# Latent projection stage with its weights loaded a stage early and eight output buffers; unused matmuls at stage borders

## The chip, the core and the metric

The kernel runs on one core of a Trainium2 chip. That core has five engines with instruction streams of their own (TensorE, called PE in the profile; VectorE, DVE; ScalarE, ACT; GpSimd, POOL; SyncE, SP, which only issues transfers), an on-chip memory of 128 partitions (SBUF), a small memory that matmuls write into (PSUM), and DMA engines between SBUF and DRAM. Engines wait for each other through semaphores. The metric is the device time of one execution in microseconds (us).

## The reference

Two transformer stacks of two layers run one after the other on one sequence of 1024 tokens, width 1024. The first has a differential attention layer, a recurrent (gated linear) layer and a squared-ReLU MLP after each. The second has two "mixed" layers, each a sum of three mixers behind one projection `h @ w_in`: retention, latent attention (MLA) and gated linear attention (GLA). What the change touches is the latent attention:

```python
q = (rms_norm(q_lat, q_norm_w) @ w_uq).reshape(b, s, MLA_HEADS, MLA_NOPE + MLA_ROPE)   # 8 heads, 64 + 32
q_nope, q_pe = q[..., :64], rope_2(q[..., 64:], pos)
kv = (rms_norm(kv_lat, kv_norm_w) @ w_ukv).reshape(b, s, MLA_HEADS, MLA_NOPE + MLA_V)
k_nope, v = kv[..., :64], kv[..., 64:]
k_pe = rope_2(k_rope[:, :, None, :], pos)[:, :, 0, :]
sc = (q_nope @ k_nope + q_pe @ k_pe) * 96 ** -0.5
mask = key_chunk[None, :] <= q_chunk[:, None]            # chunks of 64 tokens
p = softmax(where(mask, sc, -inf)); out = p @ v
```

## The kernel before

Activations lie transposed: `xT` is eight tiles of 128 channels x 1024 tokens, in SBUF all the time. The program is a row of stages: `attention_layer` (tag `da`), `trunk` (`tk`: the rest of the first stack), then for each of the two mixed layers `mixed_front` (`pj`), `mla_project` (`mp`) and `mixed_back` (`ma`), and at the end `final_norm` (`n`). Each stage allocates its buffers and semaphores with `stage(...)` and ends with a barrier over all engines (L78), so nothing of a stage starts before the last engine of the one before it, SP with its awaited stores among them, is done. Inside a stage each engine's order is written out by hand.

**`mla_project`, the stage changed most.** SP first issues the loads of `wq` (768 KB), `wk` and `wv` (256 KB each), then the rope tables and the rows of `k_rope`. PE waits for all three weights (`pe.wait_ge(sems["w"], 48)`), and then makes ten outputs of 128 x 1024 in the order `[4, 5, 0, 1, 2, 3, 6, 7, 8, 9]` into the two halves of one PSUM tile: 4 and 5 are q's rope parts, 0 to 3 q's other parts (each two plain float32 matmul steps by two halves of 512 tokens, twenty-four matmuls in all), 6 to 9 k's (one step by two halves, eight matmuls). After these come eight matmuls for v. Each float32 matmul shows as two records in the trace. ACT copies every output out of PSUM: the first two into `ab`, the next eight into `o`, and v's into `v`. `o` has two buffers, so before output number `at` >= 4 ACT waits until the stores of `at - 2` have landed (`st0`, `st1`). SP stores each output as two transfers of 64 partitions (256 KB each). After the sixth output (`at == 5`) SP waits for DVE's rotation of q's and k's rope parts and issues four more stores (two of 512 KB, two of 64 KB) before it goes on with `at` 6 to 9. At the end SP waits for all stores. `mixed_back` reads them back from DRAM.

**`mixed_back`, its first microseconds.** SP loads q (96 rows), k (64 rows) and the shared `mkpe` (32 rows) of the first pair of heads, and so on. Rows 96 to 103 of each tile hold the mask: POOL clears them for q, then for k (two memsets of 8 x 4096); DVE then writes -1e30 into q's and 1 into k's by a product with eight columns of the identity (8 instructions of 8 x 512 in all). PE's first score matmul waits for all eight (`mask` >= 8) and for the loads (`landed0`).

**`mixed_front`.** DVE scales the identity by 1/rms of each token (L386), PE multiplies that with ones to spread it over all partitions (`prep.tensor`, L355: two float32 matmuls of 512 columns), DVE then makes the normalised tiles (L403, L415) and ACT their rounded part (L337). The weights arrive in 22 panels of 512 KB through `pn.raw`, two buffers, loaded by SP (L145) and split by POOL in two parts (L160, L162, later L1183, L1185). In the second mixed layer eight column sums with one column each precede (L344), and ACT's stream begins with eight stores of `xT` and two loads. In the first the sums come from the trunk's end (L811): 16 such column sums, after DVE's last addition, before ACT and DVE make `norms` from them.

**`trunk`.** Its first panel product waits for the low parts of `oT` (L979), tile by tile.

Of the kernel before, what the change touches and what calls it, by code (L numbers as in the profile page):

```python
# [13 lines left out]
ACT = mybir.ActivationFunctionType  # L14
# [258 lines left out]
class Prep:  # L273
# [6 lines left out]
    def __init__(self, model, sems, sb, ps, chunks, size=1, eps=None, whole=False, mul=1.0, shift=None, scale=None,  # L280
                 mode="split", gates=None, sums=None, room=None, t=None, psum=None, given=None, also=None):
        self.m, self.sems, self.chunks, self.size, self.eps = model, sems, chunks, size, eps
        self.given, self.also = given, also
# [56 lines left out]
    def tensor(self, pe):  # L340
        m, sems = self.m, self.sems
        if self.whole and self.given is None:
            for b in range(SB):
                last = pe.matmul(self.stat[:, b:b + 1], m.acc[:, b * P:(b + 1) * P], m.ones[:, 0:1], start=True,  # L344
                                 stop=True)
            last.then_inc(sems["h_sums"], 1)
        for s, c in enumerate(self.normed[:1] if self.whole else self.normed):
# [9 lines left out]
            last.then_inc(sems["h_spread"], 1)  # L357

# [107 lines left out]
class Model:  # L466
# [30 lines left out]

    @contextmanager
# [42 lines left out]
    def final_norm(self, tag, name, mode):  # L541
        nc = self.nc
        with stage(nc, tag, PREP_SEMS + ["sq", "acc"]) as (sems, sb, ps):
            prep = self.norm_prep(name, 0, mode=mode)(sems, sb, ps)
# [78 lines left out]
    def trunk(self, oT, held):  # L623
# [13 lines left out]
        with stage(nc, "tk", names) as (sems, sb, ps):  # L637
# [27 lines left out]
            with nc.Block() as block:  # L665
# [62 lines left out]
                def _(pe):  # L728
# [60 lines left out]
                    pn.credit(pe)  # L789
                    linear(W_O, lambda k: pe.wait_ge(sems["o_lo"], k + 1))  # L790
# [15 lines left out]
                    mlp(1, MLP[1], 2)  # L806
                    pe.wait_ge(sems["acc"], 36)
# [5 lines left out]
                    last.then_inc(sems["n_sums"], 1)  # L813

# [287 lines left out]
    def mixed_front(self, tag, w, layer, v, o_ret, o_gla, al, make):  # L1102
# [13 lines left out]
            "l_cs", "l_kt", "l_kn", "l_s", "l_at", "l_state", "l_sm", "l_u", "l_o", "l_oc", "l_qb", "l_root", "l_rn"]  # L1116
# [4 lines left out]
        with stage(nc, tag, PANEL_SEMS + names) as (sems, sb, ps):  # L1121
# [3 lines left out]
            aux = ps("aux", [P, 2, S])  # L1125
            given = dict(given=self.norms[:, 1, :], also=self.col("fin_g", 0, DK)) if layer == 0 else {}
            prep = make(sems, sb, ps, room=ab[:, 1, 0:1, :], t=ab[:, 0, :, :], psum=aux, **given)
            pn = Panels(nc, sems, sb, ps, w, N_PROJ, DK, prep, n_v, v_parts, acc)
            decay = sb("decay", [P, 4, P])
# [32 lines left out]
            with nc.Block() as block:  # L1162
                @block.sync
                def _(sync):
# [5 lines left out]
                    pn.load(sync)  # L1170

# [39 lines left out]
                def _(pe):  # L1211
# [11 lines left out]
                    pn.credit(pe)  # L1223
                    prep.tensor(pe)
# [289 lines left out]
                def _(dve):  # L1514
# [170 lines left out]
    def mla_project(self, tag, layer, v):  # L1685
        nc = self.nc
        names = ["w", "link", "acc", "out", "st0", "st1", "tab", "kpe", "rot", "rot_st"]
        with stage(nc, tag, names) as (sems, sb, ps):
# [4 lines left out]
            wq = sb("wq", [P, 6, 2, P])  # L1693
            wk = sb("wk", [P, 4, P])
            wv = sb("wv", [P, 512])
            o = sb("o", [P, 2, S])
            acc = ps("acc", [P, 2, S])
            order = [4, 5, 0, 1, 2, 3, 6, 7, 8, 9]
            with nc.Block() as block:
                @block.sync  # L1700
                def _(sync):
                    sync.dma_start(wq[:, :, :, :].rearrange("p a b n -> p (a b n)"), self.ins["w_uq"][layer])\
                        .then_inc(sems["w"], 16)
                    sync.dma_start(wk[:, :, :].rearrange("p a n -> p (a n)"), self.ins["w_uk"][layer])\
                        .then_inc(sems["w"], 16)
                    sync.dma_start(wv[:, :], self.ins["w_uv"][layer]).then_inc(sems["w"], 16)
                    for j in range(2):
                        sync.dma_start(cs[:, j, :], self.rope2[2 + j]).then_inc(sems["tab"], 16)
                    for f in range(2):
                        sync.dma_start(ab[0:16, 1, f, :], self.proj[P_MISC, 32 * f:32 * f + 16, :])\  # L1710
                            .then_inc(sems["kpe"], 16)
                    for at, n in enumerate(order):
# [3 lines left out]
                        for hh in range(2):  # L1716

                            dst = self.mq[2 * n + hh, 0:64, :] if n < 4 else self.mk[2 * (n - 6) + hh]
                            sync.dma_start(dst, o[64 * hh:64 * hh + 64, at % 2, :]).then_inc(sems[f"st{at % 2}"], 16)
# [6 lines left out]
                    for u in range(2):  # L1726
                        sync.wait_ge(sems[f"st{u}"], 32 * 4)
# [1084 lines left out]
```

## Time and profile before

| | us |
|---|---|
| median of 3 runs (lowest, highest) | 3833.09 (3826.17, 3837.66) |
| the profiled execution's own time | 3833.74 |
| its span in the trace | 3831.8 |
| PE busy in it | 3569.6 (93%) |
| DVE, ACT, POOL busy | 1636.4, 1089.7, 1154.6 |
| mean granted clock of PE | 0.966 of full speed |

The profile is of one execution. "Busy" counts the time in which an engine's records run; in the timeline a row gives start, duration, engine, line, operation, output and inputs, and in brackets the idle time before it with what ended it. In the windows view each row is a stretch with each engine's busy time in it, PE's granted clock (1.00 is 2.4 GHz, 0.50 is 1.2 GHz), the DMA engines' busy share and what they moved. PEld is PE's weight load. "SPq" is the issue of a transfer on SP's queue.

### The profile page before, as it was taken

What the parts mean: (1) busy time and instruction counts of PE and PEld (TensorE: products, weight loads), DVE (VectorE), ACT (ScalarE), POOL (GpSimd) and SP (SyncE); (2) the same over time, 40 slices, a digit from 0 to 9 for tenths busy, and PEclk for the clock granted to TensorE, in tenths of its full rate; (3) what the DMA queues carried; (4) which work ended last, traced back from release to release, by engine and by line L of the source; (5) the groups of instructions that cost most, each with busy time, mean ns of one, the idle gap of its engine ahead of it and who ended that gap; (6) DMA issues with size and microseconds to landing.
All of it is one profiled execution on the core that took longest, in us unless ns stands there. A gap on an engine that the chain in (4) does not pass through costs nothing. (4 is left out here: it accounts for less than half of the span.)

```text
span 3831.8 us, 43821 instructions
## 1 busy us (share of the span) xinstructions
PE 3569.6 (93%) x17560; PEld 2799.0 (73%) x17560; DVE 1636.4 (43%) x1906; ACT 1089.7 (28%) x1652; POOL 1154.6 (30%) x666
## 2 busy tenths in 40 slices
PE   7999978999999999999999999799969979997897
PEld 6777756888888888788888888687625768763565
DVE  4666664312121359642111114466536431463653
ACT  2455552101010117421011011116336310443540
POOL 2554512233333346423333332232111122230211
PEclk9999988999999999999999999899989989998998
DMA  4243412111111121211111111141042121202311
GB/s 158 94 142 132 133 52 83 50 49 49 44 49 49 66 77 50 83 50 50 49 44 49 49 49 33 68 130 50 6 137 56 66 94 46 75 23 84 98 61 61
DMA packets 80124, 267.18 MB, mean 70 GB/s; under 512 B 9424, under 2 KB 10608, under 8 KB 79984
## 3 DMA queue, kind: packets, MB, share of 16 engines
q1 hardware_dynamic: 54464, 191.30, 15.3%
q10 hardware_dynamic: 18608, 48.78, 3.7%
q0 software_dynamic: 6912, 25.17, 1.9%
q8 instruction: 95, 1.56, 0.2%
q14 instruction: 45, 0.37, 0.0%
HBM read 214.62 MB, written 46.40 MB: 68 GB/s over the span
## 5 line engine op out<-in xcount | busy, mean ns | idle before, releaser
L681 POOL CAST held_hi<-held_raw 128x1024 fp32r<-128x1024 f32 x158 | 174.9, 1107 | 1182.8 <-PE tk_acc L194 646.5
L194 PE MATMUL tk_acc<-tk_b_hi,held_hi 128*128 128x512 f32 x1280 | 395.2, 390 | 8.7 <-DVE tk_b_lo L979 8.7
L194 PE MATMUL tk_acc<-tk_a_hi,held_hi 128*128 128x512 f32 x1280 | 396.1, 391 | 4.0 <-POOL held_lo L683 3.1
L194 PE MATMUL tk_acc<-tk_b_lo,held_hi 128*128 128x512 f32 x1280 | 394.9, 390 | 0.0
L194 PE MATMUL tk_acc<-tk_a_hi,held_lo 128*128 128x512 f32 x1280 | 394.9, 390 | 0.0
L194 PE MATMUL tk_acc<-tk_b_hi,held_lo 128*128 128x512 f32 x1280 | 394.9, 390 | 0.0
L194 PE MATMUL tk_acc<-tk_a_lo,held_hi 128*128 128x512 f32 x1280 | 394.6, 390 | 0.0
L683 POOL TENSOR_TENSOR held_lo<-held_raw,held_hi 128x1024 fp32r<-128x1024 f32 x158 | 385.7, 2441 | 12.7
L835 ACT ACTIVATE tk_sq<-tk_r 128x1024 f32<-128x1024 f32 x64 | 67.9, 1061 | 1067.0 <-DVE tk_r L964 1067.0
L939 DVE TENSOR_TENSOR xT<-tk_acc,xT 128x1024 f32<-128x1024 f32 x80 | 98.0, 1225 | 600.6 <-PE tk_acc L194 600.6
L194 PEld LDWEIGHTS tk_acc<-tk_b_hi,held_hi 128*128 128x128 f32 x1280 | 240.8, 188 | 59.2 <-issue 9.1
L194 PEld LDWEIGHTS tk_acc<-tk_a_hi,held_hi 128*128 128x128 f32 x1280 | 240.6, 188 | 56.1 <-POOL held_lo L683 4.8
L194 PEld LDWEIGHTS tk_acc<-tk_b_lo,held_hi 128*128 128x128 f32 x1280 | 240.8, 188 | 50.2
L194 PEld LDWEIGHTS tk_acc<-tk_b_hi,held_lo 128*128 128x128 f32 x1280 | 240.8, 188 | 50.1
L194 PEld LDWEIGHTS tk_acc<-tk_a_hi,held_lo 128*128 128x128 f32 x1280 | 240.6, 188 | 50.2
L194 PEld LDWEIGHTS tk_acc<-tk_a_lo,held_hi 128*128 128x128 f32 x1280 | 240.5, 188 | 50.2
L964 DVE SCALAR_TENSOR_TENSOR tk_r<-tk_acc,tk_rstd 128x1024 f32<-128x1024 f32 x64 | 78.4, 1224 | 393.4 <-PE tk_acc L194 393.2
L1903 PE MATMUL ma_sc<-xT 104*128 104x512 f32 (+5 forms) x384 | 154.7, 514 | 23.6 <-DVE xT L1993 22.0
L2263 POOL TENSOR_TENSOR da_mod_acc<-da_mod_acc,da_w_mod 128x1024 f32<-128x1024 f32 x42 | 115.7, 2756 | 124.2 <-ACT da_w_mod L2590 124.2
L967 DVE TENSOR_TENSOR tk_b_lo<-tk_sq,tk_b_hi 128x1024 fp32r<-128x1024 f32 x64 | 78.8, 1231 | 141.5 <-ACT tk_b_hi L837 141.5
L1960 DVE TENSOR_REDUCE ma_st<-ma_sc 128x1 f32<-128x128 f32 (+7 forms) x128 | 96.7, 755 | 85.9 <-PE ma_sc L1903 85.1
L160 POOL CAST pj_w_hi<-pj_w_raw 128x1024 fp32r<-128x1024 f32 x24 | 27.1, 1130 | 286.8 <-PE pj_acc L194 101.8
(392 smaller groups left out, 6749.9 us busy)
## 6 DMA issues: line engine op xcount, KB each, us to landing
held_raw<-in_w_trunk SPq DMA_DIRECT2D x160, 512.0 KB, 3.3
da_w_mod<-in_ada_w POOLq DMA_DIRECT2D x48, 512.0 KB, 3.9
pj_w_raw<-in_w_in SPq DMA_DIRECT2D x44, 512.0 KB, 3.3
held_raw<-in_w_qkv SPq DMA_DIRECT2D x24, 512.0 KB, 4.0
x_dram<-xT ACTq DMA_DIRECT2D x24, 512.0 KB, 4.6
ma_w_raw<-in_w_out SPq DMA_DIRECT2D x16, 512.0 KB, 3.9
xT<-x_dram SPq DMA_DIRECT2D x16, 512.0 KB, 8.4
qk_dram<-xT ACTq DMA_DIRECT2D x26, 256.0 KB
```

Of the source, the lines that this page charges most:

```text
L160: pool.tensor_copy(hi[:, u, :, :], self.raw[:, u, :, :]).then_inc(self.sems[f"w_hi{u}"], 1)
L194: last = pe.matmul(self.acc[:, u, s * HALF:(s + 1) * HALF], w[:, u, k, :], h[:, k, s * HALF:(s + 1) * HALF], start=(k == order[0] and part ...
L681: pool.tensor_copy(pn.hi[:, u, :, :], pn.raw[:, u, :, :]).then_inc(sems[f"w_hi{u}"], 1)
L683: pool.tensor_tensor(pn.lo[:, u, :, :], pn.raw[:, u, :, :], pn.hi[:, u, :, :].bitcast(F32), ALU.subtract).then_inc(sems[f"w_split{u}"], 1)
L835: act.activation(sq[:, u, :], rr, ACT.Square).then_inc(sems["sq"], 1)
L939: dve.tensor_tensor(self.xT[:, n, :], pn.acc[:, p % 2, :], self.xT[:, n, :], ALU.add)\
L964: dve.scalar_tensor_tensor(rr, pn.acc[:, u, :], 0.0, rstd[:, :], ALU.max, ALU.mult)\
L967: dve.tensor_tensor(b_lo[:, n, :], sq[:, u, :], b_hi[:, n, :].bitcast(F32), ALU.subtract)\
L1903: last = pe.matmul(dst[:, part, :], q[0:rows, u % 2, m, b * P:(b + 1) * P], k[0:rows, u % 2, m, part * w:(part + 1) * w], start=True, stop ...
L1960: dve.tensor_reduce(st[:, t % 4, 1, m:m + 1], score(m, parts, w), axis=AXXY, op=ALU.max, negate=True).then_inc(sems["neg"], 1)
L2263: pool.tensor_tensor(mod_acc[:, j % 2, :], mod_acc[:, j % 2, :], w_mod[:, n % 2, :], ALU.add).then_inc(sems["mod_added"], 1)
```

## The change

- The weights `w_uq` and `w_uk` are loaded at the end of `mixed_front` into `pn.raw`, after POOL has split the last panel, and SP waits there for their landing; `mla_project` gets that memory as `held`. Of the weights only `wv` is still loaded in `mla_project`, behind the rope tables, and PE waits for it ahead of v's matmuls.
- `o` has eight buffers; ACT's wait for stores is gone; SP counts all stores with one semaphore.
- q's mask rows are cleared (POOL) and written (DVE) in `mla_project` in `xT` rows 96 to 103, once for its four tiles; `mixed_back` does k's alone, and its first score waits for `mask` >= 4.
- `keep_busy(pe, bank, n)`: n float32 matmuls of 128 x 128 x 128 (identity by ones) into a PSUM bank that nobody reads. They stand at: the trunk's start (28), its end ahead of L811 (20) and behind it (6), the first mixed front's start (6), behind the column sums L344 of the second front and of the final norm (6 each), behind L355 in both fronts (18 each).

```diff
             for b in range(SB): ...                       # Prep.tensor, whole and given is None
             last.then_inc(sems["h_sums"], 1)
+            if self.spare is not None:
+                m.keep_busy(pe, self.spare, 6)
...
             last.then_inc(sems["h_spread"], 1)
+        if self.spare is not None and self.mode == "split":
+            m.keep_busy(pe, self.spare, 18)
...
+    def keep_busy(self, pe, bank, n):
+        for _ in range(n):
+            pe.matmul(bank, self.ident[:, :], self.ones[:, :], start=True, stop=True)
...
                     pn.credit(pe)                          # trunk
+                    self.keep_busy(pe, aux[:, 1, 0:P], 28)
                     linear(W_O, lambda k: pe.wait_ge(sems["o_lo"], k + 1))
...
                     mlp(1, MLP[1], 2)
+                    self.keep_busy(pe, aux[:, 1, 0:P], 20)
                     pe.wait_ge(sems["acc"], 36)
                     pe.wait_ge(sems["g_acc"], DK + 1)
...
                     last.then_inc(sems["n_sums"], 1)
+                    self.keep_busy(pe, aux[:, 1, 0:P], 6)
...
+            latent_w = pn.raw[:, :, :, :].rearrange("p u k n -> p (u k n)")   # mixed_front
                     pn.load(sync)
+                    for u in range(2):
+                        sync.wait_ge(sems[f"w_split{u}"], N_PROJ // 2 + 1)
+                    for src, a, b in (("w_uq", 0, 12 * P), ("w_uk", 12 * P, 16 * P)):
+                        sync.dma_start(latent_w[:, a:b], self.ins[src][layer]).then_inc(sems["latent_w"], 16)
+                    sync.wait_ge(sems["latent_w"], 32)
...
                     pn.credit(pe)
+                    if first:
+                        self.keep_busy(pe, spare, 6)
                     prep.tensor(pe)
...
-            o = sb("o", [P, 2, S])                         # mla_project
+            o = sb("o", [P, 8, S])
...
-                    sync.dma_start(wq ...), sync.dma_start(wk ...), sync.dma_start(wv ...)
                     for j in range(2):
                         sync.dma_start(cs[:, j, :], self.rope2[2 + j]).then_inc(sems["tab"], 16)
+                    sync.dma_start(wv[:, :], self.ins["w_uv"][layer]).then_inc(sems["w_uv"], 16)
...
+                @block.gpsimd
+                def _(pool):
+                    pool.memset(self.xT[96:96 + SB, 0:4, :], 0.0).then_inc(sems["clear"], 1)
...
-                        if at >= 4:
-                            act.wait_ge(sems[f"st{at % 2}"], 32 * (at // 2 - 1))
...
-                    pe.wait_ge(sems["w"], 48)
...
+                    pe.wait_ge(sems["w_uv"], 16)
                     for b in range(SB):
...
+                    dve.wait_ge(sems["clear"], 1)
+                    for u in range(4):
+                        self.mask_row(dve, self.xT[96:96 + SB, u, :], 0, NEG).then_inc(sems["mask"], 1)
+                    dve.wait_ge(sems["mask"], 4)
...
-                    for x in (q, k):                       # mixed_back
-                        pool.memset(x[kd:rows, :, :, :], 0.0).then_inc(sems["clear"], 1)
+                    pool.memset(k[kd:rows, :, :, :], 0.0).then_inc(sems["clear"], 1)
...
-                    pe.wait_ge(sems["mask"], 8)
+                    pe.wait_ge(sems["mask"], 4)
```

## Rows read from the trace of the kernel before

**Rows 1.** The page's first part: busy time, share of the span, instructions.
```profile
PE 3569.6 (93%) x17560; PEld 2799.0 (73%) x17560; DVE 1636.4 (43%) x1906; ACT 1089.7 (28%) x1652; POOL 1154.6 (30%) x666
```

**Rows 2.** Waits, whole span, then 2815 to 2842: total us, times, longest.
```profile
PE mp_acc L1752 <- DMA mp_wv<-in_w_uv: 28.9, 2, 14.5
...
PE mp_acc L1758 <- ACT mp_o L1736: 8.0, 1, 8.0
```

**Rows 3.** Timeline, latent projection of the first mixed layer.
```profile
2729.08 2.36 POOL L1185 TENSOR_TENSOR pj_w_lo<-pj_w_raw,pj_w_hi 128x1024 fp32r<-128x1024 f32 x1
...
2784.76 0.34 SPq L1702 DMA_DIRECT2D mp_wq<-in_w_uq  x1
...
2790.93 22.84 PE L1752 MATMUL mp_acc<-xT,mp_wq 128*128 128x512 f32 x48 [14.53 <-DMA mp_wv<-in_w_uv]
...
2813.81 1.02 ACT L1736 ACTIVATE mp_o<-mp_acc 128x1024 f32<-128x1024 f32 x1 [2.41 <-PE mp_acc L1752]
...
2830.33 1.02 ACT L1736 ACTIVATE mp_o<-mp_acc 128x1024 f32<-128x1024 f32 x1 [0.20 <-DMA mk_dram<-mp_o]
...
2840.34 0.59 ACT L1740 COPY mv<-mp_acc 128x512 f32<-128x512 f32 x1 [0.36 <-PE mp_acc L1758]
2841.65 0.33 SPq L1841 DMA_DIRECT2D xT<-mq_dram  x1
```

**Rows 4.** Timeline, the same stage of the second mixed layer.
```profile
3486.92 0.34 SPq L1702 DMA_DIRECT2D mp_wq<-in_w_uq  x1
...
3492.56 23.59 PE L1752 MATMUL mp_acc<-xT,mp_wq 128*128 128x512 f32 x48 [14.33 <-DMA mp_wv<-in_w_uv]
...
3532.45 1.02 ACT L1736 ACTIVATE mp_o<-mp_acc 128x1024 f32<-128x1024 f32 x1 [0.35 <-DMA mk_dram<-mp_o]
...
3542.59 0.33 SPq L1841 DMA_DIRECT2D xT<-mq_dram  x1
```

**Rows 5.** Windows view, from the sixth output to the landing of the eighth.
```profile
2816.00:2830.30 14.30, 5.02 (x12) 1.74 (x10) 0.00 (x0) 2.59 (x3) 0.00 (x0) 0.84 0.73 191
```

**Rows 6.** Start of the first mixed back: timeline, then issue to landing.
```profile
2842.74 1.05 SPq L1844 DMA_DIRECT2D xT<-mkpe_dram  x2
...
2845.19 6.06 DVE L1993 TENSOR_SCALAR xT<-ident 8x512 f32<-8x512 f32 x8 [29.92 <-POOL xT L1859]
...
2851.31 7.89 PE L1903 MATMUL ma_sc<-xT 104*128 104x512 f32 x12 [11.00 <-DVE xT L1993]
...
xT<-mkpe_dram SPq DMA_DIRECT2D x2, 128.0 KB, 7.2
```

**Rows 7.** Timeline, float32 matmuls of 128 columns, at the lower and the upper clock.
```profile
541.90 3.59 PE L2385 MATMUL da_ov<-da_v,da_pts 128*128 128x128 f32 x16 [0.71 <-ACT da_pts L2579]
...
549.01 1.60 PE L2385 MATMUL da_ov<-da_v,da_pts 128*128 128x128 f32 x12 [0.50 <-ACT da_pts L2579]
```

**Rows 8.** Windows view, PE's granted clock behind two kinds of stream.
```profile
545.40:547.00 1.60, 1.60 (x9) 0.72 (x9) 0.50 (x2) 0.00 (x0) 0.00 (x0) 0.95 0.00 0
...
2403.26:2410.20 6.94, 6.94 (x32) 6.87 (x32) 0.00 (x0) 0.00 (x0) 0.00 (x0) 0.50 0.00 0
```

**Rows 9.** Timeline, first products of the trunk.
```profile
598.22 1.19 PE L194 MATMUL tk_acc<-tk_b_hi,held_hi 128*128 128x512 f32 x2 [8.73 <-DVE tk_b_lo L979]
...
603.48 0.68 PE L194 MATMUL tk_acc<-tk_b_hi,held_hi 128*128 128x512 f32 x2
```

**Rows 10.** Timeline, from the trunk's last sums into the first mixed front.
```profile
2403.26 3.54 PE L811 MATMUL tk_aux<-ones,acc 128*128 128x1 f32 x16 [4.89 <-DVE tk_rstd L1090]
...
2415.48 3.78 PE L355 MATMUL pj_aux<-pj_ab,ones 128*128 128x512 f32 x4 [5.26 <-DVE pj_ab L386]
...
2437.72 0.38 PE L220 MATMUL pj_acc<-pj_w_hi,m_h_hi 128*128 128x256 f32 x1 [2.76 <-DVE m_h_lo L415]
```

**Rows 11.** Timeline, second mixed front, then the final norm.
```profile
3118.45 1.28 ACT L321 ACT_TABLE_LOAD   x1 [14.79 <-issue]
...
3809.60 3.78 PE L355 MATMUL n_h_spread<-n_h_diag,ones 128*128 128x512 f32 x4 [1.85 <-DVE n_h_diag L386]
```

More of the change, by code:

```diff
@@ L543, in final_norm @@
         with stage(nc, tag, PREP_SEMS + ["sq", "acc"]) as (sems, sb, ps):
[L544 removed]
+            prep = self.norm_prep(name, 0, mode=mode)(sems, sb, ps, spare=ps("spare", [P, P])[:, :])
             sq = sb("sq", [P, 2, S])
@@ L1681, in _, with mask_row, mla_project @@
                         dve.tensor_tensor(o_gla[:, j, :], o_gla[:, j, :], ab[:, 0, j, :], ALU.mult)
-    def mla_project(self, tag, layer, v):
+        return latent_w
+    def mask_row(self, dve, rows, first, value):
+        dst = rows.rearrange("p (b n) -> p b n", b=SB)[:, :, first:first + 64]
+        eye = self.ident[96:96 + SB, 96:96 + SB].rearrange("p (b n) -> p b n", n=1)
+        return dve.tensor_scalar(dst, eye.broadcast_to([SB, SB, 64]), value, None, ALU.mult)
+    def mla_project(self, tag, layer, v, held):
         nc = self.nc
-        names = ["w", "link", "acc", "out", "st0", "st1", "tab", "kpe", "rot", "rot_st"]
+        names = ["w_uv", "link", "acc", "out", "st", "tab", "kpe", "rot", "rot_st", "clear", "mask"]
         with stage(nc, tag, names) as (sems, sb, ps):
@@ L1725, in _ @@
                                 sync.dma_start(self.mkpe[f], ab[0:16, 1, f, :]).then_inc(sems["rot_st"], 16)
-                    for u in range(2):
-                        sync.wait_ge(sems[f"st{u}"], 32 * 4)
+                    sync.wait_ge(sems["st"], 32 * 8)
                     sync.wait_ge(sems["rot_st"], 64)
+                @block.gpsimd
+                def _(pool):
+                    pool.memset(self.xT[96:96 + SB, 0:4, :], 0.0).then_inc(sems["clear"], 1)
                 @block.scalar
@@ L1985, in low @@
                                           ALU.subtract).then_inc(sems["o_lo"], 1)
-                    for x, first, value in ((q, 0, NEG), (k, 64, 1.0)):
-                        dve.wait_ge(sems["clear"], 1 if x is q else 2)
-                        for u in range(2):
-                            for m in range(2):
-                                dst = x[kd:rows, u, m, :].rearrange("p (b n) -> p b n", b=SB)[:, :, first:first + 64]
-                                eye = self.ident[kd:rows, kd:rows].rearrange("p (b n) -> p b n", n=1)
-                                dve.tensor_scalar(dst, eye.broadcast_to([SB, SB, 64]), value, None, ALU.mult)\
-                                    .then_inc(sems["mask"], 1)
+                    dve.wait_ge(sems["clear"], 1)
+                    for u in range(2):
+                        for m in range(2):
+                            self.mask_row(dve, k[kd:rows, u, m, :], 64, 1.0).then_inc(sems["mask"], 1)
                     for u in range(2):
```

26 lines of the change are left out of this document (11 added, 15 removed).

## The prediction, made before the changed kernel ran

> **What bounds the kernel now.** The page's first part comes first: PE is busy for 93% of the span [rows 1], so elsewhere only what leaves PE idle or slow is to be had, some 262 us in all. The windows view by hundreds of microseconds then shows where: nearly all of the trunk is full at clock 1.00, and the gaps lie at the stage borders. The list of waits names the largest of one line: PE waited 28.9 us, twice, for the last of the three weight loads of the latent projection [rows 2]. The timeline of that stage shows its order. In the first mixed layer the stage begins at 2784.8, PE starts at 2790.93, ACT, held by the landing of a store, copies its last `o` at 2830.33, its last copy ends at 2840.93, and the next stage begins at 2841.65, 0.7 us behind [rows 3]. Inside it PE stood 8.0 us for ACT [rows 2], which had no free buffer. So PE with ACT sets this stage's end, and two things make it late: the weights, and two output buffers. The second layer repeats it: 3486.92, 3492.56, 3532.45, 3542.59 [rows 4].
>
> **Part 1, weights out of the stage.** PE starts with the stage: 2790.93 - 2784.8 = 6.1 us earlier, 5.6 in the second layer [rows 3, 4]. The loads' new place is SP's queue in the front, behind its last panel load; nothing is queued behind them but the stage's end. POOL's last split there ends at 2731.44, some 50 us before that end, against the 6.1 us that all three took here [rows 3], so I cost it at nothing; without that cover it would cost about those 6. ACT's copies, DVE's rotation and SP's stores follow PE, and move by the same 6.1 us: the rope tables are now first in the queue, so they don't hold DVE.
>
> **Part 2, eight buffers.** ACT's waits go. What is late next? PE and ACT took 2840.93 - 2790.93 = 50.0 us; less the 8.0 us of waiting this is 42.0, so they would end by 2784.8 + 42.0 = 2826.8, earlier still where v's matmuls don't start at the lower clock. The stores do not go away. The sixth output was ready at 2814.83 [rows 3]; from there to the landing of the eighth at 2830.33 the queue was never empty, and it moved 191 GB/s [rows 5]. All that moves 6.1 us forward, to 2824.2. Two outputs of 512 KB remain, 1.05 MB, now queued right behind: at 191 GB/s 5.5 us. SP sees the last store at 2829.7, and the next stage begins 0.7 us later, at 2830.4 instead of 2841.65: **11.2 us** less. In the second layer 3532.45 - 5.6 + 5.5 + 0.7 = 3533.1 against 3542.59: **9.5 us**. So the stores become the bound, some 3 us and more behind PE and ACT, and part of what PE gains is idle time again. Bounds: nothing but part 1's 5 us per layer if the deeper queue slows the stores a little, 18 per layer if the stores keep up (first rival).
>
> The page "SBUF — State Buffer" of the Trainium skill (section on the DMA port swizzle) says that a transfer from 64 partitions reaches only half of SBUF's DMA ports, worth 218 GB/s by its figures. The trace's 191 GB/s agrees with that. [...]
>
> **Part 3, mask rows.** In the back stage DVE's eight mask writes (6.06 us, 0.76 each) end at 2851.25 and release PE at 2851.31. DVE began 3.5 us after the stage, behind POOL's first memset. Without q's, POOL clears once and DVE writes four: ready at 2841.65 + 3.5 + 3.0 = 2848.2. But the loads of `mkpe` were issued from 2842.74 on and took 7.2 us: the second landed at about 2850.5 [rows 6]. So PE starts 0.7 us earlier, not 3.0, and in the second layer about as much, of which I take 0.4: **1.1 us**. Bounds 0 and 6.1. In the projection the four writes (3.0 us) and one memset end long before the stores.
>
> **Part 4, unused matmuls.** One of them is two records. 16 records at the lower clock took 3.59 us, 12 at the upper 1.60 [rows 7]: 0.21 and 0.12 us a record, so 0.43 and 0.24 us a matmul. Can such matmuls raise the clock? After the 3.59 us of 128-column matmuls it stood at 0.95; 6.9 us of one-column matmuls, PE busy throughout, left it at 0.50 [rows 8]. So I take it that fillers do it and column sums don't.
>
> [...]
>
> - Trunk's end. 20 fillers start warm behind the last product and take 4.8 us, about the 4.89 us for which PE waits for DVE anyhow [rows 10]: no delay. The 32 records of column sums took 6.94 us at 0.50 [rows 8]; at full clock half, 3.5. I take 3.2, since the clock may fall inside them. The chain over `norms` and the barrier hangs on them: **3.2 us** (bounds 0 and 3.5). The 6 behind (1.4 us) are shorter than that chain.
> - First front. L355 took 3.78 us at 0.50 [rows 10]; warm 1.9. Behind it DVE's normalised tiles are what PE waits for (2.76 us before 2437.72), so a gain there counts, and POOL, which slows DVE beside it, may turn 1.9 into 2.6 or 0. Whether the clock is still up after the border is even. I take **1.0** (bounds 2.6 gained, 0.5 lost by 6 cold fillers).
> - Trunk's start. PE is idle 8.73 us before 598.22, and the 5.3 us after it run at half speed, which costs 2.6 [rows 9]. 28 fillers from 591.4 on: about 4.5 us cold (10 of them), 18 warm, 4.3 us; they end at 600.2, 2.0 late, and give back 2.6. **0.4** net (bounds 2.6 gained, 5.2 lost).
> - Second front. L355 there waits for ACT, whose own stores and loads hold it to 3118.45 [rows 11]; fillers at either end lie in idle time, PE then waits for DVE's tiles. Zero (0.5 either way).
> - Final norm. 6 fillers at the lower clock take 2.6 us where PE has 1.85 free, 0.8 late; L355's 3.78 us may end faster for it. Zero (0.9 gained, 0.8 lost) [rows 11].
>
> **Sum.** 11.2 + 9.5 + 1.1 + 3.2 + 1.0 + 0.4 = 26.4 us. The profiled execution took 3833.74, with 1.9 us around its span; it lies 0.65 above the median of the three runs. 3833.7 - 26.4 = 3807.3, so I say 3807.
>
> **Rivals.**
> 1. *The stores keep up.* For it: the two halves of an output lie in different partitions and can run together. Against it: they were in the queue together before, at 191 GB/s [rows 5]. Then PE and ACT set the end, some 37 us after the stage's start with v's matmuls warm: 18.9 and 17.6 instead of 11.2 and 9.5, total 42.2: 3792. Chance 0.17.
> 2. *The fillers don't raise the clock, or too late.* 28 cold ones take 12 us and delay the trunk by 5.2; the front's lose 0.5, the final norm's 0.8, the column sums gain nothing. 26.4 - 3.2 - 1.4 - 0.4 + 6.5 would leave 15.3 to 16: 3818. For it: the one-column rows. Against it: the clock after 128-column ones. Chance 0.17.
> 3. *Crowded stores, the slower side.* From the sixth output on 3.75 MB are to be stored. Before, ACT's waits spaced them; now they queue from 2808.7 on. If the rate fell to 118 GB/s, the stage would end where it did; at 90 GB/s the last lands 41.7 us later, 2850.4, and the two stages lose about 9 each: 3833.7 + 18 - 5.7 = 3846. For it: nothing but the deeper queue; against it: the same rate with four stores queued. Chance 0.03.
> 4. *It doesn't do what it says:* something else holds PE at the stage's start (code, the barrier), so part 1 fails: 11 us less gain, 3818. Chance 0.06.
>
> The forecast has 0.57. Bounds of the forecast itself are 3800 to 3814. About 0.3% (11.5 us) is what a measurement of this kernel can tell from no change; 3821.6 is that border. The first rival and the forecast are clear of it, the second and fourth by 3 to 4 us, so a fifth of them falls inside: faster 0.91, same 0.06, slower 0.03. The range takes in half of the first rival and most of the second and fourth: 3794 to 3818.
>
> **What would show it.** After: no load ahead of PE in `mp`, its first matmul at the stage's start; ACT without waits for a DMA there; SP's last wait for `mk_dram` ending the stage, PE idle some 3 us or more before it; the first scores released by a load, not by L1993's successor; L811's records at half their length; first trunk product near 600.2 (shifted by nothing before it) at clock 1.00. I am wrong if the latent stages end with PE or ACT, if they are not about 46 us long (57 before), or if the trunk starts its products after 602.

## The result and the profile after

The changed kernel took 3804.74 us (median of 4 runs, 3804.07 to 3808.10) against 3831.02 (3826.17 to 3837.66) for the kernel before in the same comparison: ratio 0.993, 95% interval 0.9918 to 0.9941, 26.3 us by the medians. The profiled execution has a span of 3806.3 us (before 3831.8). The page's first part stands beside that of [rows 1]; PE has 216 records more, the unused matmuls.

```profile
PE 3589.7 (94%) x17776; PEld 2828.3 (74%) x17776; DVE 1630.1 (43%) x1906; ACT 1089.5 (29%) x1652; POOL 1157.8 (30%) x666
```

Cut at the first instruction of each stage (the trunk's at its first ACTq issue), the two spans compare so, in us:

| stage | before | after | gain | predicted |
|---|---|---|---|---|
| first attention (unchanged) | 591.4 | 596.5 | -5.2 | 0 |
| trunk | 1821.9 | 1820.3 | 1.6 | 3.6 |
| front 1, front 2 | 371.5, 381.1 | 370.7, 380.4 | 0.8, 0.7 | 1.0, 0 |
| latent 1, latent 2 | 56.9, 55.7 | 44.3, 43.5 | 12.6, 12.2 | 11.2, 9.5 |
| back 1, back 2 | 264.2, 262.1 | 263.7, 260.5 | 0.5, 1.6 | 1.1 together |
| final norm | 27.1 | 26.5 | 0.7 | 0 |

The largest gain is where it was looked for. The latent stage of the first mixed layer, timeline (start, duration, engine, line, operation; beside [rows 3]):

```profile
2787.57 0.80 SPq L1730 DMA_DIRECT2D mp_cs<-rope_dram  x2
...
2787.61 30.31 PE L1775 MATMUL mp_acc<-xT,pj_w_raw 128*128 128x512 f32 x64 [8.41 <-PEq L78]
...
2818.54 9.59 SPq L1742 DMA_DIRECT2D mk_dram<-mp_o  x8
...
2825.60 0.58 ACT L1764 COPY mv<-mp_acc 128x512 f32<-128x512 f32 x1 [0.35 <-PE mp_acc L1782]
...
2831.83 1.28 ACT L2050 ACT_TABLE_LOAD   x1 [5.64 <-PEq L78]
```

PE starts with the stage and makes all 64 records without a gap. ACT's last copy ends at 2826.18, and then nothing runs for 5.64 us: SP's stores of k's outputs, issued until 2828.1, are the end. The second layer's stage, with its first row and the first of the next stage, leaves the same gap, 5.98 us:

```profile
3475.93 0.81 SPq L1730 DMA_DIRECT2D mp_cs<-rope_dram  x2
...
3519.39 1.28 ACT L2050 ACT_TABLE_LOAD   x1 [5.98 <-PEq L78]
```

The windows view of the changed kernel shows what the first layer's stores moved (stretch, busy time of PE, PEld, DVE, ACT, POOL with record counts, PE's clock, DMA share, GB/s):

```profile
2801.80:2813.00 11.20, 11.20 (x27) 4.94 (x26) 11.06 (x12) 3.28 (x5) 0.00 (x0) 1.00 0.55 140
2813.00:2818.50 5.50, 5.50 (x14) 2.28 (x12) 1.03 (x4) 3.42 (x4) 0.00 (x0) 1.00 0.75 169
2818.50:2831.50 13.00, 6.81 (x15) 2.16 (x14) 0.00 (x0) 5.06 (x9) 0.00 (x0) 0.96 0.72 221
```

Start of the first back stage (beside [rows 6]): DVE's four writes take 1.44 us in place of 6.06 for eight, and what releases PE is a load.

```profile
2835.36 1.44 DVE L1710 TENSOR_SCALAR xT<-ident 8x512 f32<-8x512 f32 x4 [21.34 <-POOL xT L1886]
...
2840.96 8.19 PE L1930 MATMUL ma_sc<-xT 104*128 104x512 f32 x12 [15.40 <-DMA xT<-mkpe_dram]
```

Both ends of the trunk, and the first front (beside [rows 9, 10]):

```profile
596.88 8.70 PE L505 MATMUL tk_aux<-ones,ident 128*128 128x128 f32 x56 [2.20 <-PEq L78]
605.33 0.71 PE L194 MATMUL tk_acc<-tk_b_hi,held_hi 128*128 128x512 f32 x2
...
2403.17 4.63 PE L505 MATMUL tk_aux<-ones,ident 128*128 128x128 f32 x40
2408.22 1.92 PE L822 MATMUL tk_aux<-ones,acc 128*128 128x1 f32 x16 [0.43 <-DVE tk_rstd L1102]
2410.00 3.05 PE L822 MATMUL tk_aux<-ones,tk_rstd 128*128 128x1 f32 x16
2412.91 2.91 PE L505 MATMUL tk_aux<-ones,ident 128*128 128x128 f32 x12
2417.22 2.90 PE L505 MATMUL pj_acc<-ones,ident 128*128 128x128 f32 x12 [1.41 <-PEq L78]
2419.92 2.33 PE L357 MATMUL pj_aux<-pj_ab,ones 128*128 128x512 f32 x4
```

The first product comes 8.79 us behind the stage's start (6.85 before), but at the upper clock at once: its two records take 0.71 us, not 1.19. At the other end the first sixteen records of the column sums ran in 1.92 us, the next sixteen in 3.05: the clock fell inside them. The six unused matmuls behind took 2.91 us, and the next stage begins 3.8 us behind the sums in place of 3.05.

### The profile page after: what moved, and what is told of

Its sections match the earlier page's. It is cut to its first block and busy times, and to the rows that moved or that the text cites. A ratio compares the mean times of both kernels' runs of the same rounds, so it can differ in the third digit from the quotient of the medians.

```text
span 3806.3 us, 44249 instructions
## 1 busy us (share of the span) xinstructions
PE 3589.7 (94%) x17776; PEld 2828.3 (74%) x17776; DVE 1630.1 (43%) x1906; ACT 1089.5 (29%) x1652; POOL 1157.8 (30%) x666
```

## Experiments

Each kernel below the first was timed in five rounds against the kernel before. The last two columns are the lengths of the two latent stages in its one profile. They did not all run on one chip, so the ratio to the kernel before, and not the median, compares them. How far a stage length can be trusted is shown by kernels with the same code in that stage: 56.9 and 56.1, 55.7 and 57.2 us (before, unused matmuls only), 44.3, 44.7 and 43.6, 43.5, 44.0 and 44.5 (changed, no unused matmuls, q's mask in the back). So 1 us, and 1.5 us in the second layer before, is chance.

| kernel | median | ratio, 95% interval | latent 1 | latent 2 |
|---|---|---|---|---|
| changed kernel | 3804.7 | 0.9930, 0.9918 to 0.9941 | 44.3 | 43.5 |
| no unused matmuls | 3811.7 | 0.9955, 0.9940 to 0.9970 | 44.7 | 44.0 |
| unused matmuls only | 3825.3 | 0.9999, 0.9988 to 1.0010 | 56.1 | 57.2 |
| two buffers | 3818.0 | 0.9972, 0.9958 to 0.9986 | 50.9 | 51.8 |
| weights in the stage | 3817.8 | 0.9969, 0.9957 to 0.9981 | 50.3 | 50.6 |
| k before q | 3805.2 | 0.9927, 0.9911 to 0.9944 | 40.6 | 41.1 |
| k in 128 partitions | 3803.1 | 0.9925, 0.9910 to 0.9941 | 42.2 | 43.9 |
| q's mask in the back | 3810.9 | 0.9935, 0.9918 to 0.9951 | 43.6 | 44.5 |
| two queues | 3815.7 | 0.9950, 0.9933 to 0.9968 | 46.8 | 47.9 |
| all stores in 128, trimmed | 3854.9 | 1.0062, 1.0044 to 1.0081 | 69.5 | 69.5 |
| k before q, trimmed | 3799.7 | 0.9913, 0.9895 to 0.9930 | 41.1 | 41.1 |
| the 128 one with back fill | 3854.4 | 1.0064, 1.0048 to 1.0079 | 70.0 | 70.1 |
| combined | 3796.2 | 0.9901, 0.9882 to 0.9919 | 40.0 | 41.3 |

### Without the unused matmuls, and with them alone

```diff
-        for _ in range(n):
+        for _ in range(0):
```

> The changed kernel without any of its unused matmuls. My theory: nearly all of the gain sits in the two latent stages (44.3 and 43.5 us long in the changed kernel, 56.9 and 55.7 before) and the mask rows; the unused matmuls bring 3 to 4 us. So 3808 to 3809 against 3804.7 for the changed kernel, the two latent stages unchanged at 44.3 and 43.5. Rival (the unused matmuls also lift later stretches, as the last back stage that got 1.6 us shorter): 3810 or more, and that stage back at 262.1 us. Rival (they don't pay): 3804 or less.

> The kernel before with nothing but the unused matmuls, at the same places. My theory: 3 to 4 us faster than before (trunk's end 1.4, fronts 0.8 and 0.7, final norm 0.6, trunk's start 0.1), 3827 to 3828 against 3831; the trunk's first product about 8.8 us behind the stage's start at clock 1.00. The prediction's own terms give 4.6. Rival 2 of the prediction (cold matmuls that only delay): slower than before. If the last back stage gets 1.6 us shorter here too, the unused matmuls are its cause.

The latent stages kept their length without them (44.7, 44.0). The total, 3811.7, and the last back stage, 264.1 us, are the first rival's figures (3810 or more, 262.1), not mine. But that stage also took 264.0 us with the unused matmuls alone, and 261.5 to 264.8 in the six other kernels that have all of them (262.1 before). So they don't shorten it, and the 260.5 of the changed kernel's profile was chance. By stages the unused matmuls bring 3.2 and 3.0 us in the two pairs: changed against without, trunk 1.3, fronts 0.7 and 0.2, norm 1.0; alone against before, trunk 1.9, first front 1.4, second -0.5, norm 0.4. The trunk is the surest of these: 1820.0 to 1820.5 us in all eight profiles with the full set, 1821.6 and 1821.9 in the two without. The total can't tell it: alone they have a ratio of 0.9999 with some 4 us either way, so the loss that the second rival of the prediction wanted isn't excluded by the time, only by the places in the trace. The first back stage was 262.5 us without any and 259.3 with them alone. Alone, the first front's six ran warm, as the profile of the kernel with nothing but them shows, and the spread matmuls in 1.98 us:

```profile
2409.64 1.58 PE L505 MATMUL pj_acc<-ones,ident 128*128 128x128 f32 x12 [1.38 <-PEq L78]
2411.50 1.98 PE L357 MATMUL pj_aux<-pj_ab,ones 128*128 128x512 f32 x4 [0.29 <-DVE pj_ab L390]
```

### Two buffers; weights in the stage

```diff
-            o = sb("o", [P, 8, S])
+            o = sb("o", [P, 2, S])
...
+                        if at >= 4:
+                            act.wait_ge(sems[f"st{at % 2}"], 32 * (at // 2 - 1))
```

> The changed kernel with o back at two buffers and ACT's waits for the stores (weights still loaded in the front). My theory: the stage is that of before moved forward by PE's earlier start, 56.9 - 6.1 = 50.8 and 55.7 - 5.6 = 50.1 us; ACT waits for stores again; total 13 us above the changed kernel, near 3818. Rival (the stores bound the stage either way, and buffers bring nothing): 44.3 and 43.5 us, total 3805. Rival (weights bring nothing by themselves, since ACT's waits for stores take it up): 56 us, total 3829.

```diff
+                    sync.dma_start(held[:, 0:12 * P], self.ins["w_uq"][layer]).then_inc(sems["w_uv"], 16)
+                    sync.dma_start(held[:, 12 * P:16 * P], self.ins["w_uk"][layer]).then_inc(sems["w_uv"], 16)
...
+                    pe.wait_ge(sems["w_uv"], 48)
```

> The changed kernel with eight buffers, but its weights loaded in the stage, ahead of the rope tables, PE waiting for all three as before. My theory: every output and so every store comes 6.1 (second layer 5.6) us later, and the stage follows in full: 50.4 and 49.1 us, total 3816 to 3817. Rival (the end is set by stores whose queue is empty for part of the time, so a later start is partly caught up): 47 to 49 us, total about 3811. Rival (the early loads themselves cost time in the front, where they end it later): the fronts 370.7 and 380.4 us get shorter by more than 0.5 us.

The rivals of both fell. With two buffers the stages are 50.9 and 51.8 us (50.8 and 50.1 expected): early weights are worth 6.0 and 3.9 against before, and the buffers 6.6 and 8.3 on top. With the weights in the stage they are 50.3 and 50.6 (50.4 and 49.1 expected): early weights are worth 6.1 and 7.2 on top of eight buffers, the buffers alone 6.6 and 5.1. In the first layer each part is worth the same with and without the other, so there they add up. In the second they come to 9.0 of 12.2 us. Half of that difference hangs on the 55.7 of the profile before: against the 57.2 of the same code with unused matmuls, early weights are worth 5.4 and the buffers 6.6. The kernel with two buffers shows the wait, ACT's copies of k's outputs held by landings, and PE's v matmuls behind them:

```profile
2805.25 1.02 ACT L1763 ACTIVATE mp_o<-mp_acc 128x1024 f32<-128x1024 f32 x1 [2.72 <-DMA mq_dram<-mp_o]
2814.91 1.02 ACT L1763 ACTIVATE mp_o<-mp_acc 128x1024 f32<-128x1024 f32 x1 [8.63 <-DMA mk_dram<-mp_o]
...
2816.08 10.22 PE L1785 MATMUL mp_acc<-mp_wv,xT 128*128 128x512 f32 x16 [7.76 <-ACT mp_o L1763]
```

The fronts, with the loads gone from their end, were 371.4 and 380.8 us long and not shorter than 370.7 and 380.4, so the early loads cost nothing there, against the second rival. In the stage, PE waited for the loads again, 5.9 us from its start:

```profile
2792.85 30.37 PE L1773 MATMUL mp_acc<-xT,pj_w_raw 128*128 128x512 f32 x64 [14.20 <-DMA mp_wv<-in_w_uv]
```

### Is it the rate of the stores? k before q

```diff
-            order = [4, 5, 0, 1, 2, 3, 6, 7, 8, 9]
+            order = [4, 5, 6, 7, 8, 9, 0, 1, 2, 3]
...
-                        if at == 5:
+                        if at == 7:
```

> The changed kernel with k's four outputs made between the rope parts and q's others, and the rope stores issued two outputs before the last. Same work, same bytes; stores start about as early, but the cheap outputs fill the queue first, while PE makes the dear ones. My theory (the stores' rate bounds the stage's end): from the first stored output (12.5 us behind the stage's start) 5.4 MB at about 190 to 200 GB/s end 40.5 to 41.5 us behind it; stages of 41 to 42 us instead of 44.3 and 43.5, 4 to 5 us in all. Rival (what counts is the time of the last outputs, not the rate): the last output of 128 x 1024 now comes at the same place of PE's stream, stages stay at 44 us. Rival (the end is PE and ACT): nothing moves either.

The stages took 40.6 and 41.1 us: 3.7 and 2.4 us less with the same work and bytes, and 40.0 to 41.3 in both later kernels with this order. The bound by stores is shown, not only argued. k's outputs now fill the time in which PE makes q's, when the changed kernel's queue moved 140 GB/s (first window above). In this kernel:

```profile
2793.40:2801.00 7.60, 7.60 (x19) 3.42 (x18) 7.53 (x7) 3.16 (x4) 0.00 (x0) 1.00 0.77 232
...
2811.80:2821.50 9.70, 6.76 (x15) 2.17 (x14) 0.00 (x0) 5.01 (x9) 0.00 (x0) 1.00 0.65 188
```

ACT's last copy ended at 2819.45, the next stage began at 2821.77: 2.3 us are left of 5.6.

### The form of the stores

```diff
+                        if n >= 6:
+                            dst = self.mk[2 * (n - 6):2 * (n - 6) + 2].rearrange("m d s -> (m d) s")
+                            sync.dma_start(dst, o[:, at - 2, :]).then_inc(sems["st"], 16)
```

> The changed kernel with each of k's outputs stored as one transfer from 128 partitions (512 KB) instead of two from 64. Theory A (a transfer from 64 partitions is the limit, and two of them don't add up): k's 2.1 MB go at up to twice the rate, the end falls to PE and ACT, stages of 39.5 to 40.5 us, 8 us in all. Theory B (the two halves already run side by side, the rate is that of the queue or of the engines): 44.3 and 43.5 us as in the changed kernel, within 1 us. The page SBUF - State Buffer of the Trainium skill, section on the DMA port swizzle, has 64 partitions reach half of the ports; by that rule alone theory A holds.

The stages took 42.2 and 43.9 us: 2.0 us less in one layer, 0.4 more in the other, of which about 1 us can be chance. Theory A wanted 4 in both, so its times fell; nor does B hold within its 1 us in the first layer. The rate tells more. In the last six microseconds of the stream, first and second layer, the one transfer moved 366 and 357 GB/s:

```profile
2814.00:2820.00 6.00, 3.95 (x9) 1.19 (x8) 0.00 (x0) 2.95 (x6) 0.00 (x0) 1.00 0.93 366
2820.00:2822.00 2.00, 0.00 (x0) 0.00 (x0) 0.00 (x0) 0.00 (x0) 0.00 (x0) 0.99 0.14 57
3496.00:3502.00 6.00, 3.80 (x9) 1.12 (x8) 0.00 (x0) 2.93 (x5) 0.00 (x0) 1.00 0.92 357
3502.00:3505.00 3.00, 0.00 (x0) 0.00 (x0) 0.00 (x0) 0.00 (x0) 0.00 (x0) 0.94 0.11 46
```

The changed kernel's pairs of halves moved 288 and 272 in theirs:

```profile
2824.00:2830.00 6.00, 1.56 (x4) 0.30 (x2) 0.00 (x0) 1.55 (x3) 0.00 (x0) 1.00 0.90 288
3511.00:3517.00 6.00, 1.79 (x4) 0.31 (x3) 0.00 (x0) 1.75 (x3) 0.00 (x0) 0.96 0.89 272
```

So the one transfer is the faster form by a quarter and more, as theory A has it: in the first layer the bulk was through 39 us behind the stage's start, not 42. The stage ended late all the same: for 2 and 3 us behind the stream only some two of sixteen DMA engines' worth still moved (share 0.14 and 0.11), and the stages ended 4.4 and 5.3 us behind ACT's last copy. Why a few engines lagged, no run shows. And in the kernel without unused matmuls, a stretch of stores by halves of 64 partitions moved 310:

```profile
2821.00:2824.00 3.00, 0.74 (x2) 0.00 (x0) 0.00 (x0) 1.00 (x2) 0.00 (x0) 1.00 0.88 310
```

So halves in the queue together do pass the 218 GB/s that the Trainium skill's page "SBUF — State Buffer" (DMA port swizzle) gives to a transfer of 64 partitions; the measurement decides, and that figure is at most the price of a half by itself.

```diff
-                        for hh in range(2):
+                        for hh in range(2 if n < 4 else 1):
...
+                        act.dma_start(self.mk[2 * (order[at] - 6) + 1], o[64:128, at - 2, :]).then_inc(sems["st"], 16)
```

> The changed kernel with the second half of each of k's outputs stored from ACT's queue instead of SP's. Theory A (one queue's depth is the limit: SP's issues are held back, 9.59 us for eight): two queues carry more, stages of 40 to 41 us, 6 to 8 us in all. Theory B (the DMA engines or SBUF's side are the limit): 44 and 43.5 us, within 1 us. The cost of four issues on ACT (some 0.5 us each) lies in ACT's idle time.

The stages took 46.8 and 47.9 us, 2.5 and 4.5 us longer. Neither theory had that. The profile of this kernel shows ACT's issues held back for up to 3.23 us, with v's copies and so PE behind them, and SP's rope stores taking 4.32 us to issue:

```profile
2814.67 4.32 SPq L1746 DMA_DIRECT2D mq_dram<-mp_ab  x1
...
2815.71 3.23 ACTq L1760 DMA_DIRECT2D mk_dram<-mp_o  x1
...
2823.73 5.64 PE L1790 MATMUL mp_acc<-mp_wv,xT 128*128 128x512 f32 x10 [0.43 <-ACT mv L1772]
```

Windows view of the same kernel:

```profile
2813.00:2821.00 8.00, 6.17 (x15) 2.32 (x13) 0.49 (x2) 3.37 (x4) 0.00 (x0) 1.00 0.81 182
```

The rate stayed near the changed kernel's (182 GB/s here, then 212 over 6 us, against 169 and then 221 there), so the second queue brought no rate, and a second engine was held up. The page "DMA: Bandwidth & Descriptors" of the Trainium skill (section on issuing engines) says that all issuers share the same DMA engines, so that more issuers save issue time at most; the trace agrees, and adds that the issue itself can hold up the engine that makes it (3.23 us).

### q's mask rows back in the back stage

```diff
-                    pool.memset(k[kd:rows, :, :, :], 0.0).then_inc(sems["clear"], 1)
+                    for x in (q, k):
+                        pool.memset(x[kd:rows, :, :, :], 0.0).then_inc(sems["clear"], 1)
```

> The changed kernel with q's mask rows cleared and written in the back stage again, as before. My theory: the first score matmul starts 9.6 to 9.7 us behind the back stage's start instead of 9.1 and 9.3, released by DVE; 0.3 to 0.5 us a layer, nothing that the total can show. Rival (part 3 is worth what DVE's writes and POOL's clearing take, 3 us a layer): 12 us behind. Rival (the loads are the bound anyway, it is worth nothing): 9.1 and 9.3.

The first score started 9.66 and 9.65 us behind the stage's start, released by DVE, in place of 9.14 and 9.33: 0.5 and 0.3 us. My figures held; neither rival did.

```profile
2834.78 6.06 DVE L1710 TENSOR_SCALAR xT<-ident 8x512 f32<-8x512 f32 x8 [22.68 <-POOL xT L1879]
...
2840.90 4.64 PE L1923 MATMUL ma_sc<-xT 104*128 104x512 f32 x5 [15.78 <-DVE xT L1710]
```

The view by line of this kernel, the shortest, middle and longest of these eight writes in ns, explains the 6.06:

```profile
L1710 DVE TENSOR_SCALAR xT<-ident x8: 409/416/3698, 2834.8 to 2840.4; 8x512 f32<-8x512 f32 x8
```

One write, the first, took 3.70 us, as long as POOL's second memset ran beside it, and the other seven about 0.41 each. In the kernel before it is the same (409, 416 and 3697). So 0.76 us each is a mean over one write that stood still and seven quick ones.

### Combinations, and how many unused matmuls

```diff
-                    self.keep_busy(pe, aux[:, 1, 0:P], 28)
+                    self.keep_busy(pe, aux[:, 1, 0:P], 20)
...
-                    self.keep_busy(pe, aux[:, 1, 0:P], 6)
...
-                    if first:
-                        self.keep_busy(pe, spare, 6)
...
+                        dst = self.mq[2 * n:2 * n + 2, 0:64, :] if n < 4 else self.mk[2 * (n - 6):2 * (n - 6) + 2]
+                        sync.dma_start(dst, o[:, at - 2, :]).then_inc(sems["st"], 16)
```

> Changed kernel with k's outputs before q's, every output stored as one transfer from 128 partitions, 20 unused matmuls at the trunk's start instead of 28, none behind the trunk's last column sums, none at the first front's start. My theory: latent stages at PE's and ACT's own length, 39 to 40.5 us; trunk's first product 6.9 us behind the stage's start instead of 8.8, its clock at 1.00 soon after, so the trunk stage 1816.0 - 1.9 - 0.8 = 1813.3; the first front within 0.5 of 370.7. Some 10 us faster than the changed kernel, 3794 to 3796 on the same chip. Rival (without the 6 and 6 the first front's spread matmuls L357 fall back to the lower clock, 3.8 us instead of 2.3): the front 1 us longer. Rival (the trunk's 28 are needed for the clock): the first products at 0.50, stage 1816.

The latent stages took 69.5 us, 30 more than I said, and the kernel became slower than the one before. With all engines done, the last stores, of q's outputs, went on for 26 us:

```profile
2817.00:2843.00 26.00, 0.00 (x0) 0.00 (x0) 0.00 (x0) 0.00 (x0) 0.00 (x0) 0.50 0.13 53
```

A DMA share of 0.13 is two engines of sixteen, and 53 GB/s is what two moved. `mq` has 96 rows a head, of which 64 are written, so the target falls in two pieces; `mk`'s target is one unbroken block. The page "DMA: Bandwidth & Descriptors" of the Trainium skill (section on why a DMA increments its semaphore by 16) says that the number of engines is the largest up to 16 that divides the slowest dimension of both sides, here 2; the row agrees. I had counted the source's partitions alone.

The trunk's first product came as I said: 6.75 us behind the stage's start in place of 8.79, at the upper clock, and the next stage 3.04 us behind the sums in place of 3.8. The stage took 1816.9 us, 3.4 less than the changed kernel's 1820.3, where I had said 2.7. My 1813.3 is out by more, as it set out from 1816.0, which is not that kernel's length. The first front was 371.1 us, 0.4 longer, its spread matmuls at 3.75 us: a loss, but half of what the rival wanted, and within what this stage varies by.

```profile
587.33 6.12 PE L505 MATMUL tk_aux<-ones,ident 128*128 128x128 f32 x40 [2.29 <-PEq L78]
593.65 0.70 PE L194 MATMUL tk_acc<-tk_b_hi,held_hi 128*128 128x512 f32 x2 [0.20 <-DVE tk_b_lo L990]
```

The next kernel has `28` made `12`, none of the six behind the sums, k before q, stores as in the changed kernel:

> The same, but outputs stored as two transfers of 64 partitions each, 12 unused matmuls at the trunk's start and the first front's 6 kept. My theory: latent stages 40.6 to 41.1 as with k first alone; the 12 (5.2 us cold, 24 records) are short of raising the clock for good: they end 1.6 us before the first product, which starts 6.9 us behind the stage's start as before; clock either kept (2.6 us gained) or lost again. Behind the trunk's column sums the stage ends 0.8 to 1.0 us earlier, as DVE's norms and not PE's unused matmuls end it.

Twelve were enough for the clock. They ended 1.4 us before the first product, which ran at the upper clock all the same (0.70 us for two records); trunk stage 1818.6 (1816.9, 1817.1 and 1818.3 in the three kernels with 20), latent stages 41.1 as with k first alone.

```profile
598.46 5.05 PE L505 MATMUL tk_aux<-ones,ident 128*128 128x128 f32 x24 [2.20 <-PEq L78]
604.93 0.70 PE L194 MATMUL tk_acc<-tk_b_hi,held_hi 128*128 128x512 f32 x2 [1.43 <-DVE tk_b_lo L990]
```

Then unused matmuls in the back stages, where PE waits for loads:

```diff
+                    self.keep_busy(pe, ov[:, 1, 0:P], 26)
                     pe.wait_ge(sems["mask"], 4)
```

> The first of these three with 26 unused matmuls more at the start of each back stage, where PE is idle for 9.1 us until the first loads land. My theory: they end before the loads do (10 cold at 0.43 and 16 warm at 0.24 us, 8.1 us), the first scores run at 1.00 instead of 0.50, and DVE's second maximum, 16.1 us behind the stage's start, comes 2 us earlier: 1 to 2 us a layer. Rival (DVE and ACT, not PE, pace the first blocks): under 0.5 us. Rival (the clock also matters further on, since PE is not busy throughout in these stages, 258 to 265 us long from run to run): 3 us a layer or more.

DVE's second maximum of the first back stage came 12.8 us behind its start, 16.1 in the changed kernel: 3.3 us at that place, more than the 2 that I said. The stage was 258.9 us, the second 261.2 (263.8 and 262.0 in the kernel without this fill). But first back stages of 258.3 and 259.3 us occur without it, so a gain for the stage isn't shown.

> Changed kernel with k's outputs before q's, k's stored as one transfer from 128 partitions into one unbroken block of DRAM, q's as two transfers of 64 again; 20 unused matmuls at the trunk's start, none behind its column sums nor at the first front's start; 26 at the start of each back stage. My theory: q's stores as one transfer with a target in two pieces made the stages of 69 us, nothing else; so latent stages of 40 to 41 us, trunk stage 3.4 us shorter than in the changed kernel, the first back stages' second maximum 3.3 us earlier. 3.5 + 2.7 + 3.4 + 6 = some 16 us faster than the changed kernel: 3786 to 3791. Rival (k's stores too were hurt by being one transfer, or k before q was): latent stages above 42 us. Rival (the back stages' 3.3 us are lost again later): 3793 to 3797.

```profile
2784.80 29.42 PE L1774 MATMUL mp_acc<-xT,pj_w_raw 128*128 128x512 f32 x64 [8.41 <-PEq L78]
...
2821.90 0.59 ACT L1763 COPY mv<-mp_acc 128x512 f32<-128x512 f32 x1 [0.36 <-PE mp_acc L1781]
2824.79 0.33 SPq L1868 DMA_DIRECT2D xT<-mq_dram  x1
...
3506.11 6.04 PE L505 MATMUL ma_ov<-ones,ident 128*128 128x128 f32 x52 [2.92 <-PEq L78]
3515.67 6.87 PE L1930 MATMUL ma_sc<-xT 104*128 104x512 f32 x8 [3.51 <-DMA xT<-mkpe_dram]
```

0.9901 (0.9882 to 0.9919), the lowest ratio of all; 3796.2 us is the second rival's figure (3793 to 3797), not mine (3786 to 3791). Latent stages 40.0 and 41.3, trunk 1818.3: the target in two pieces was the whole of the 30 us. In the first layer the fill worked (scores warm, stage 259.2). In the second it started warm, ended 3.5 us too early, PE fell back, the scores ran cold, and the stage took 264.3. The interval just touches the changed kernel's (0.9918 to 0.9941), so this version beats the kernel before for sure, the changed kernel probably.

## Why the prediction was right, step by step

**Sum.** 3807 against 3804.74; 26.4 us against 26.3 by the medians. The mechanism was right, but the nearness is in part luck. In the profiled pair all stages but the first gained 30.7 us by the table, 4.1 of them more than forecast in the latent stages, and the unchanged first stage lost 5.2. That stage ended between 586.3 and 598.1 us in fourteen profiles with the same code.

**Part 1, weights.** Predicted 6.1 and 5.6. Measured 6.0 and 3.9 without the buffers, 6.1 and 7.2 with them (the second layer's differ by chance as much as its 55.7 and 57.2 before); nothing for the loads' new place. The step held, PE starting 0.04 us behind the stage.

**Part 2, buffers.** The term that was mis-sized. I had 11.2 and 9.5 for both parts, so 5.1 and 3.9 for this one; measured 6.6 and 8.3 on top of part 1. "The stores become the bound, some 3 us and more behind PE and ACT": they did, 5.6 us behind ACT's last copy. PE and ACT ended 38.6 us behind the stage's start and not 42: v's matmuls ran warm, as I had named as possible, and PE's other wait for ACT, 1.3 us before, went too. That only widened the idle gap, it isn't in the sum. What is in the sum is the price of two more outputs at 191 GB/s, and it was too high: the last 13 us moved 221, the last six 288. The 191 [rows 5] is from a stretch in which ACT, with two buffers, fed the queue only as stores landed, and "the queue was never empty" is not so at its ends: the DMA engines' share was 0.09 from 2814.8 to 2816 and 0.04 to nothing from 2829.5 to 2831. Right behind that stretch, in the same stage of the kernel before, the last two outputs, the very ones that I priced, went at 245:

```profile
2831.00:2835.00 4.00, 4.00 (x6) 1.58 (x5) 0.00 (x0) 1.53 (x3) 0.00 (x0) 0.50 0.86 245
```

The stages became 44.3 and 43.5 us, not 45.6 and 46.2; by my own sign ("about 46 us long") the second was a miss by 2.7.

**Part 3, mask rows.** Predicted 0.7 and 0.4, measured 0.5 and 0.3, the release by a load as said. DVE's four writes took 1.44 us and not 3.0: my 0.76 each was a mean over a first write that stood 3.70 us beside POOL's second memset and seven of some 0.41. That changes nothing here, the loads being the later ones.

**Part 4, unused matmuls.** They do raise the clock, and column sums don't; the second rival's premise fell, though the first front's six ran cold in the changed kernel (2.90 us) and warm alone (1.58). Trunk's start: product 1.94 us late, 2.0 predicted, with the first products at the upper clock at once, which was to give back 2.6; what is left of the trunk's 1.6 us beside its end is 0.2 (0.4 forecast). The sign "after 602" was in the time of the profile before: the product came at 605.3 because the stage itself began 5.2 us later. Trunk's end: 3.2 predicted, about 1.4 measured. Of it the sums gained 2.1, and the step that failed is "the 6 behind (1.4 us) are shorter than that chain": the clock fell inside the column sums, which I had allowed for in the sums only, so the six took 2.91 us and held the stage's end by 0.75 us. First front: 0.8 for 1.0. Second front and norm: 0.7 and 0.7 for zero. In the two pairs of experiments the second front shows 0.2 and -0.5, so nothing that can be told from chance, the norm 1.0 and 0.4; the norm's spread matmuls ran in 1.96 us for 3.78 [rows 11]. Of the whole part, 4.6 predicted, the two pairs of experiments show 3.2 and 3.0.

**Rivals.** The first, stores that keep up, is out: ACT was done 5.6 us before the end, and k before q moved the end. Its remark that two halves run together was right in part, though (288 to 310 GB/s, the one transfer 366), and with the low price of the stores goes the forecast for the latent stages, which was too low. The second's sum has a wrong sign: its 6.5 us are losses, so 26.4 - 3.2 - 1.4 - 0.4 - 6.5 leaves 14.9. The third (crowded stores) fell: the deeper queue moved more, not less. The fourth fell with PE's first matmul.

**Open.** Whether the second layer gained more from buffers and from early weights than the first: one profile each, and the same code differs by up to 1.5 us there. Why a few DMA engines lagged behind the stream when k's outputs went as one transfer, which ate part of what its rate gave in one layer and all of it in the other. That it is POOL's memset which holds DVE's first write rests on their ending together, in three stages alike; no run left the second memset alone out.

## What to carry to other kernels

When a wait for buffers goes, ask what the freed stream runs into, and find its rate in a stretch where nothing but that stream set the pace: not the 191 GB/s of a queue that was fed by landings, but the 245 right behind it. A stage that still ends with its stores once it has buffers enough was shortened here by the order of its outputs (the cheap ones first, so that the queue is fed while the dear ones are made), and made longer by a second queue. Unused matmuls paid here where their end met the start of real work; in front of a barrier, behind one-column sums, they were the last thing that the stage waited for. A mean over eight instructions can hide one that stood still: look at the longest.

## What the runs showed of the hardware

- One transfer of 128 source partitions whose target falls in two pieces ran at 53 GB/s with a DMA share of 0.13; the same bytes as two transfers ran, with the rest of that stretch, at 188 (k before q).
- Stores of 512 KB from 128 partitions moved 366 and 357 GB/s over 6 us, the same bytes as pairs of 64 partitions 288 and 272. Behind the first kind some two engines' worth of transfer went on for 2 to 3 us.
- A second issuing queue for half of k's stores made the stage 2.5 to 4.5 us longer.
- A DVE write of 8 x 512 took 3.70 us beside a POOL memset and some 0.41 without one.
- After unused matmuls PE kept the upper clock over 1.4 us of idle time, at the trunk's start, and had lost it after 3.5 us, in the combined kernel's second back stage. Inside 4.8 us of column sums at the trunk's end, busy throughout, it fell.
- The same code differs by several us from run to run where PE is not busy throughout, and the granted clock goes with it. Rows of the first attention stage in the changed kernel, and, from another kernel, with the same code there (k in 128 partitions):

```profile
500.00:550.00 50.00, 39.82 (x189) 26.82 (x190) 28.61 (x52) 22.46 (x50) 2.94 (x1) 0.73 0.06 21
```

```profile
500.00:550.00 50.00, 38.58 (x230) 25.99 (x230) 31.52 (x60) 25.98 (x59) 0.00 (x0) 0.90 0.06 22
```

The first kernel's trunk began at 596.5 us, the second's at 588.6.
